# Half of x's channel pairs come from DRAM as 32x32 blocks and are turned by DVE; TensorE turns the other half

## The chip, the cores and the metric

The kernel runs on one core of a Trainium2 chip. The metric is the device time of one execution, in microseconds (us), as the median of three runs.

The engines are named as the profile names them: PE (TensorE, with PEld for its weight loads), ACT (ScalarE), DVE (VectorE), POOL (GpSimd) and SP (SyncE, which here only issues DMAs). Each works through its own instructions in the order in which they are written, and semaphores tie them together.

## What is computed

A hybrid layer for 256 tokens and 4096 channels in float32: a norm, one wide projection, three mixers (a gated mLSTM, a sparse attention, a gated delta rule), and an output projection that is added to x.

```python
h = rms_norm(x, norm_g[l])
proj = jnp.einsum('bsd,dn->bsn', h, w_in[l])
(aq, ak, av, ai, af, ao, az,
 bcq, bk, bv, bki, bwi, bz,
 cqkv, cb, ca, cz) = jnp.split(proj, split_points, axis=-1)
...
y = jnp.concatenate([y_a, y_b, y_c], axis=-1)
x = x + jnp.einsum('bsm,md->bsd', y, w_out[l])
```

What concerns the change is only how x comes to stand as the stationary operand of the first matrix multiplication: with channels on the 128 partitions and tokens along the free dimension. In DRAM x lies the other way round, tokens by channels.

## The kernel before, in words

All weights are streamed once from DRAM in **chunks** of 128 channels by 1024 numbers (512 KB, two groups of 128 channels by 512 columns). Each chunk goes through three engines. SP loads it into `w_raw` (four buffers). ACT copies it, rounded to a shorter float, into `w_hi` (`split_hi`). DVE subtracts to get the remainder `w_lo` (`split_lo`). PE then multiplies in three products, `hi*hi`, `hi*lo` and `lo*hi`, which makes twelve matmuls of 128x512 per chunk (lines 825 to 827). Sixteen chunks make one block of 512 output columns; the blocks follow each other to the end of the kernel, and the mixers' work is woven in between their chunks.

The operand of these matmuls, `op_hi` and `op_lo`, holds h transposed, 32 groups of 128 channels by 256 tokens. It is made during the first block. This stretch, from the start to about 59 us, is called the **x phase** here. x is loaded by SP in pieces into `xs`, tokens on partitions. For each pair of channel groups i (16 pairs, one for each chunk of the first block), four steps follow:

- `x_columns(i)` on PE: four transposes of 128x128 from `xs` into a PSUM bank `mix` (they appear as line 798);
- `x_hi(i)` on ACT: two copies of 128x256 from the bank, times the norm's gain, into `op_hi` (line 1391);
- `x_lo(i)` on DVE: two operations of 128x256 that read the bank and `op_hi` and write `op_lo` (line 1915);
- chunk i on PE, which waits for `x_lo(i)` and for `split_lo(i)`.

The order on each engine is fixed by the loops over chunks c. On PE it is `chunk(c)`, then `x_columns(c + 2)`. On ACT it is `x_hi(c + 2)`, `split_hi(c + 3)`, `x_square(c)` (a square of 128x512 with a running sum, for the norm). On DVE it is `x_lo(c + 2)`, `split_lo(c + 3)`. One round of the loops is called a **slot**, and slot i is the one in which ACT runs `x_hi(i)`, then `split_hi(i + 1)`. `split_hi(c)` also waits for the load of chunk c and for PE to have finished chunk c - 4; SP issues the load of chunk c when `split_lo(c - 4)` is done.

POOL makes a few constants in the first 5 us and then has nothing to do until the first block is finished; after that it moves tiles through DRAM scratch in blocks of 32x32 numbers (`keep_blocks`, `bring_blocks`), and DVE turns those blocks in place (`STREAM_TRANSPOSE`). The scratch moves of `conv`, `v`, `lane` and the others are of this kind.

Of the kernel before, what the change touches and what calls it, by code (L numbers as in the profile page):

```python
# [17 lines left out]
ACT = mybir.ActivationFunctionType  # L18
AX_X = mybir.AxisListType.X

P = 128
D = 4096
SEQ = 256
# [45 lines left out]
AHEAD = SPLIT_BUFS - 1  # L69
X_AHEAD = 2  # L70
NX = KT // 2
X_PARTS = [(q, q + SEQ) for q in range(0, 1024, SEQ)] + [(q, q + 512) for q in range(1024, D, 512)]
WARM = (2, 2, 1)
RSQRT = 1597463007.0
# [150 lines left out]
def hybrid_kernel(nc, x, norm_g, w_in, w_out, m_ib, m_fb, m_norm_g, a_cq_g, a_wuq, a_wuqi, a_qn_g, a_kn_g,  # L225
                  a_ki_g, a_ki_b, d_conv_w, d_a_log, d_dt_bias, d_norm_g, out):
    blocks, chunks, last, woven, _ = plan()
    U0 = NX + 1

    matrix = {  # L230
        "w_in": w_in[0].rearrange("(kt p) n -> p kt n", p=P),
# [7 lines left out]
    with ExitStack() as ctx:  # L239
# [3 lines left out]
        def sem(name):  # L243
            return ctx.enter_context(nc.semaphore(name))
# [11 lines left out]
        op_hi = sb("op_hi", [P, KT, SEQ], F32R)  # L256
        op_lo = sb("op_lo", [P, KT, SEQ], F32R)
# [89 lines left out]
        x_ready = [sem(f"x_ready{q}") for q in range(len(X_PARTS))]  # L347
        raw_ready = [sem(f"raw_ready{b}") for b in range(RAW_BUFS)]
        const_ready = sem("const_ready")
        pool_step = sem("pool_step")  # L350
        head_ready = sem("head_ready")
        x_hi_ready = sem("x_hi_ready")
# [115 lines left out]
        def first_half(tensor, i):  # L468
            w = blocks[0]["width"]
            return tensor[:, 0, i * w:i * w + w]  # L470

        def first_bank(j):

# [11 lines left out]
        def bank(use):  # L485
            return mix[use % 4]

        def wait_filled(eng, use):
            eng.wait_ge(filled[use % 4], use // 4 + 1)
# [116 lines left out]
        def _(pool):  # L606
# [24 lines left out]
            for i, lv in enumerate(MERGES):  # L631
                b = 1 << lv
# [3 lines left out]
                select(v, ALU.is_ge, 0.0, -b, [[-2 * b, n], [0, b]], 1)  # L636
                select(v, ALU.is_ge, 0.0, 2 * b - 1, [[2 * b, n], [0, b]], -1)
            nc.gpsimd.engine_nop().then_inc(const_ready, 1)

            def clear_corners(m):  # L640

# [151 lines left out]
        def _(pe):  # L793
# [6 lines left out]
            def chunk(c):  # L800
                b, kts = chunks[c]
                blk = blocks[b]
                w = blk["width"]
                if kts[0] == blk["kts"][0] and b >= 2:
                    pe.wait_ge(acc_read[b % 2], b // 2)
                pe.wait_ge(lo_ready, c + 1)
                hi, lo = {"h": (op_hi, op_lo), "cq": (cq_hi, cq_lo), "y": (op_hi, op_lo)}[blk["operand"]]
                hv = split_ap(w_hi, c).rearrange("p (k n) -> p k n", k=len(kts))
                lv = split_ap(w_lo, c).rearrange("p (k n) -> p k n", k=len(kts))
                if c == len(chunks) - 1:  # L810
                    order = [(i, kt, [m]) for m in range(M) for i, kt in enumerate(kts)]
                else:
                    order = [(i, kt, range(M)) for i, kt in enumerate(kts)]
                for i, kt, ms in order:
                    if b == 0:
                        use = 1 + kt // 2
                        pe.wait_ge(emptied[use % 4], use // 4 + 1)
                    if blk["operand"] == "cq":
                        pe.wait_ge(cq_lo_ready, kt // 2 + 1)
                    if blk["kind"] in ("out1", "out2") and blk["arg"] == 0:  # L820
                        pe.wait_ge(y_lo_ready, (kt // 2 + 12) % 16 + 1)
                    for m in ms:
                        o = acc[b % 2][m][:, 0:w]
                        tok = slice(m * P, m * P + P)
                        nc.tensor.matmul(o, hi[:, kt, tok], hv[:, i, :], start=(kt == blk["kts"][0]), stop=False)  # L825
                        nc.tensor.matmul(o, hi[:, kt, tok], lv[:, i, :], start=False, stop=False)  # L826
                        last_mm = nc.tensor.matmul(o, lo[:, kt, tok], hv[:, i, :], start=False,  # L827
                                                   stop=(kt == blk["kts"][-1]))
                        if c == len(chunks) - 1 and m == 0 and kt == kts[-1]:
                            last_mm.then_inc(last_half, 1)  # L830
                if c == last[b]:
                    last_mm.then_inc(acc_ready, 1)
                    pe_done[0] += 1
                else:
                    last_mm.then_inc(split_used, 1)
# [201 lines left out]
            def second_chunk(c):  # L1037

                w = blocks[0]["width"]
                hv = split_ap(w_hi, c).rearrange("p (k n) -> p k n", k=2)  # L1040
                lv = split_ap(w_lo, c).rearrange("p (k n) -> p k n", k=2)
                use = 1 + c
                pe.wait_ge(emptied[use % 4], use // 4 + 1)
                pe.wait_ge(hi_ready, c + 1)
                for part, op in ((hv, op_hi), (hv, op_lo), (lv, op_hi)):
                    if part is lv:
                        pe.wait_ge(lo_ready, c + 1)
                    for i in range(2):
                        for m in range(M):
                            ins = nc.tensor.matmul(acc[0][m][:, 0:w], op[:, 2 * c + i, m * P:m * P + P],  # L1050
                                                   part[:, i, :], start=False, stop=False)
                ins.then_inc(split_used, 1)
# [4 lines left out]
                    nc.tensor.matmul(bank(3)[:, 0:P], ident[:], ident[:], start=True, stop=True)  # L1057

            def x_columns(i):
                use = 1 + i  # L1060
                pe.wait_ge(x_ready[i if i < 4 else i // 2 + 2], 16)
                wait_emptied(pe, use)
                for j in range(2):
                    for m in range(M):
                        o = first_bank(j) if i == 0 else bank(use)[:, j * SEQ:j * SEQ + SEQ]
                        ins = turn(o[:, m * P:m * P + P], xs[:, m, (2 * i + j) * P:(2 * i + j) * P + P])
                    if i == 0 and j == 0:
                        ins.then_inc(first_turned, 1)
                end_fill(ins, use)
# [12 lines left out]
            for c in range(1, len(chunks)):  # L1082
                if c < 3:
                    second_chunk(c)
                else:
                    chunk(c)
                if c + X_AHEAD < NX:
                    x_columns(c + X_AHEAD)
                if c == NX:
                    pe.wait_ge(const_ready, 2)  # L1090
                for name, arg, use in woven[c]:
                    if name in pieces:
                        pieces[name](arg, U0 + use)


        @block.scalar
        def _(act):
# [286 lines left out]
                          bs=bs, bp=bp, ae=ae, ap=ap, yt=yt)  # L1384

            def x_hi(i):
                use = 1 + i
                wait_filled(act, use)
                for j in range(2):
                    kt = 2 * i + j  # L1390
                    ins = func(op_hi[:, kt, :], bank(use)[:, j * SEQ:j * SEQ + SEQ], ACT.Copy,
                               scale=par[:, R_NORM + kt:R_NORM + kt + 1])
                ins.then_inc(x_hi_ready, 1)

            def x_square(i):
                q, m = i // M, i % M
                for part in ((0, 1), (2, 3))[q] if q < 2 else (q + 2,):
                    act.wait_ge(x_ready[part], 16)
                func(y[:, m, 512 * q:512 * q + 512], xs[:, m, 512 * q:512 * q + 512], ACT.Square,
                     accum_out=ssq[:, m, q:q + 1]).then_inc(ss_ready, 1)  # L1400

            def first_x(j):
# [43 lines left out]
        def _(dve):  # L1446
# [9 lines left out]
            def done_bank(ins, use):  # L1456
                ins.then_inc(emptied[use % 4], 1)
# [443 lines left out]
            def par_columns(_, use):  # L1901
                for i, (c0, n) in enumerate(((R_CQ, R_N - R_CQ), (R_N, N_TAP))):
# [4 lines left out]
                          co=co, cy=cy, bn=bn, bt=bt, bkn=bkn, bkt=bkt, bit=bit, bqn=bqn, bqt=bqt, bsc=bsc, btk=btk, bts=bts, bs=bs, bo=bo, at=at, ae=ae, ap=ap, ay=ay,  # L1907
                          yd=yd, yt=yt)

            def x_lo(i):  # L1910
                use = 1 + i
                dve.wait_ge(x_hi_ready, i + 1)
                for j in range(2):
                    kt = 2 * i + j
                    ins = vec.scalar_tensor_tensor(op_lo[:, kt, :], bank(use)[:, j * SEQ:j * SEQ + SEQ],
                                                   par[:, R_NORM + kt:R_NORM + kt + 1], op_hi[:, kt, :].bitcast(F32),
                                                   ALU.mult, ALU.subtract)
                done_bank(ins, use)

            wait_filled(dve, 0)  # L1920
            done_bank(vec.tensor_copy(par[:, 0:R_CQ], bank(0)[:, 0:R_CQ]), 0)
# [14 lines left out]
            for c in range(len(chunks)):  # L1936
                if 0 < c < NX - X_AHEAD:
                    x_lo(c + X_AHEAD)
                if c + AHEAD < len(chunks):
                    split_lo(c + AHEAD)  # L1940
                if c == NX - 1:
                    dve.wait_ge(ss_ready, NX)
                    step(vec.tensor_reduce(rstd[:], ssq[:], AX_X, ALU.add))
                    rsqrt_mean(rstd[:], D, rstd_ready)
                    dve.wait_ge(const_ready, 2)
                for name, arg, use in woven[c]:
                    if name in pieces:
                        pieces[name](arg, U0 + use)
# [26 lines left out]
```

## Time and profile before

| | us |
|---|---|
| median of three runs | 1555.44 |
| lowest and highest | 1554.95, 1555.63 |
| the profiled execution's own time | 1556.13 |
| its span, first to last instruction | 1554.4 |

PE's clock is granted in full over the whole span (the page shows 9, that is 90% or more, in each of 40 slices). The profile's rows are read as: start, duration, engine, line, what is written from what, count; in brackets the idle time ahead of the row and what ended it. A row with x2 or x4 covers that many instructions, and its duration is their total. Instructions of one engine overlap by about 0.1 us, so the distance between two starts is the time that the first one takes of its engine. The groups have the busy time in us, the mean duration of one in ns, and the idle time ahead of them.

### The profile page before, as it was taken

How to read it: one execution, taken by the hardware profiler on the slowest of the kernel's cores; microseconds unless marked ns; L12 is line 12 of the kernel's file. 1: busy time of each engine (PE TensorE's matmuls, PEld its weight loads, DVE VectorE, ACT ScalarE, POOL GpSimd, SP SyncE). 2: the span in 40 equal slices, each digit the busy share in tenths (PEclk: the TensorE clock that was granted, in tenths of full speed). 3: DMA queues.
4: the chain of work that ended last, by engine and by line, in shares of the span. 5: the costliest groups of instructions: out<-in, count | busy, mean ns of one | idle time of the engine just before them, and what ended most of it. 6: DMA issues, size and time to landing. Idle time of an engine off the chain costs nothing.

```text
span 1554.4 us, 18886 instructions
## 1 busy us (share of the span) xinstructions
PE 1548.2 (100%) x7124; PEld 1281.0 (82%) x7124; DVE 979.9 (63%) x1503; ACT 757.6 (49%) x1022; POOL 292.8 (19%) x492
## 2 busy tenths in 40 slices
PE   9999999999999999999999999999999999999999
PEld 7888888888888888888878888888888888888887
DVE  5665555666759854566579666665456776665554
ACT  6654444487544444554545545544445444444332
POOL 0121112230020030026610241333500110100000
PEclk9999999999999999999999999999999999999999
DMA  8677778886687675468856765676875766666674
GB/s 295 209 211 219 214 221 225 211 234 193 200 231 209 196 218 157 130 189 271 257 182 180 221 211 174 211 234 202 281 214 179 256 205 196 202 206 194 193 250 153
DMA packets 179095, 327.74 MB, mean 211 GB/s; under 512 B 29346, under 2 KB 34612, under 8 KB 178876
## 3 DMA queue, kind: packets, MB, share of 16 engines
q1 hardware_dynamic: 161324, 284.00, 60.7%
q0 software_dynamic: 17632, 42.52, 9.6%
q8 instruction: 56, 0.92, 0.2%
q14 instruction: 35, 0.29, 0.1%
q10 hardware_dynamic: 48, 0.02, 0.0%
HBM read 307.05 MB, written 19.42 MB: 210 GB/s over the span
## 4 chain that ended last, share of the span: by engine, by line
PE 97%; DVE 1%; ACT 1%; issue 0%; DMA 0%; ACTq 0%
PE acc L825 31%; PE acc L827 30%; PE acc L826 30%; PE mix L897 1%; PE mix L798 1%; PE mix L981 1%; PE mix L879 0%; DVE w_lo L1462 0%; PE mix L962 0%; PE acc L1050 0%; ACT w_hi L1120 0%; PE mix L959 0%; PE mix L949 0%; PE mix L947 0%; PE mix L991 0%
## 5 line engine op out<-in xcount | busy, mean ns | idle before, releaser
L1462 DVE TENSOR_TENSOR w_lo<-w_raw,w_hi 128x1024 fp32r<-128x1024 f32 (+2 forms) x535 | 645.9, 1217 | 427.7 <-ACT w_hi L1120 424.1
L825 PE MATMUL acc<-w_hi,op_hi 128*128 128x512 f32 (+1 forms) x2036 | 802.5, 394 | 0.3 <-DVE w_lo L1462 0.3
L1120 ACT ACTIVATE w_hi<-w_raw 128x1024 fp32r<-128x1024 f32 (+2 forms) x535 | 556.0, 1050 | 504.7 <-PE acc L827 452.9
L827 PE MATMUL acc<-w_hi,op_lo 128*128 128x512 f32 (+1 forms) x2036 | 793.4, 390 | 0.0
L826 PE MATMUL acc<-w_lo,op_hi 128*128 128x512 f32 (+1 forms) x2036 | 792.3, 389 | 0.0
L827 PEld LDWEIGHTS acc<-w_hi,op_lo 128*128 128x128 f32 x2036 | 382.1, 188 | 81.0
L825 PEld LDWEIGHTS acc<-w_hi,op_hi 128*128 128x128 f32 x2036 | 382.4, 188 | 80.4 <-DVE w_lo L1462 2.7
L826 PEld LDWEIGHTS acc<-w_lo,op_hi 128*128 128x128 f32 x2036 | 382.5, 188 | 76.6
L650 POOL DMA_DIRECT2D y_dram<-y x64 | 41.0, 713 | 211.1 <-DVE y L1877 115.2
L650 POOL DMA_DIRECT2D conv_dram<-y x48 | 30.9, 703 | 207.5 <-ACT y L1172 206.8
L650 POOL DMA_DIRECT2D bq_dram<-qs x32 | 20.4, 676 | 158.4 <-DVE qs L1751 157.9
L658 POOL DMA_DIRECT2D y<-y_dram x64 | 33.9, 538 | 34.5 <-DMA y_dram<-y 34.0
L1344 ACT ACTIVATE b_p<-b_s,st 128x128 f32<-128x128 f32 (+1 forms) x32 | 14.3, 446 | 52.9 <-DVE st L1824 52.9
L825 PE MATMUL acc<-w_hi,cq_hi 128*128 128x512 f32 x84 | 33.7, 401 | 0.0
L826 PE MATMUL acc<-w_lo,cq_hi 128*128 128x512 f32 x84 | 33.1, 394 | 0.0
L827 PE MATMUL acc<-w_hi,cq_lo 128*128 128x512 f32 x84 | 33.1, 394 | 0.0
L658 POOL DMA_DIRECT2D y<-conv_dram x48 | 25.5, 542 | 22.9 <-DMA conv_dram<-y 22.9
L1593 DVE SCALAR_TENSOR_TENSOR cT<-y,par,cT 128x255 f32<-128x255 f32 (+2 forms) x72 | 29.4, 476 | 0.0
L788 POOL DMA_DIRECT2D out_dram<-acc x2 | 1.5, 731 | 124.6 <-DVE acc L1485 124.6
L711 POOL DMA_DIRECT2D lane_out_dram<-lane_u x4 | 4.2, 1068 | 108.2 <-DVE lane_u L1651 108.2
L1651 DVE TENSOR_TENSOR lane_u<-lane_u,lane_t 128x252 f32<-128x252 f32 (+52 forms) x63 | 22.4, 356 | 2.2
L1222 ACT ACTIVATE cT<-cT 128x512 f32<-128x512 f32 x12 | 7.6, 633 | 33.1 <-DVE cT L1593 33.1
(326 smaller groups left out, 927.3 us busy)
## 6 DMA issues: line engine op xcount, KB each, us to landing
w_raw<-in_w_in_dram SPq DMA_DIRECT2D x367, 512.0 KB, 4.4
w_raw<-in_w_out_dram SPq DMA_DIRECT2D x128, 512.0 KB, 4.6
w_raw<-in_w_in_dram SPq DMA_DIRECT2D x16, 384.0 KB, 3.2
w_raw<-in_a_wuq_dram SPq DMA_DIRECT2D x12, 512.0 KB, 4.9
y_dram<-y POOLq DMA_DIRECT2D x64, 64.0 KB, 4.2
y<-y_dram POOLq DMA_DIRECT2D x64, 64.0 KB, 3.5
xs<-in_x_dram SPq DMA_DIRECT2D x6, 512.0 KB, 5.1
conv_dram<-y POOLq DMA_DIRECT2D x48, 64.0 KB, 3.8
```

The costliest lines, as they stand in the source:

```text
L650: pool.dma_start(dst[:, :, :, 4 * m + i, :].rearrange("a k j b -> a (k j) b"), src[32 * i:32 * i + 32, m].rearrange("p (f b) -> p f b", b= ...
L658: pool.dma_start(dst[32 * j:32 * j + 32, q].rearrange("p (k t) -> p k t", k=2), src[:, 2 * q:2 * q + 2, j].rearrange("a k i b -> a k (i b) ...
L798: return nc.tensor.transpose(dst, src, ident[0:n, 0:n])
L825: nc.tensor.matmul(o, hi[:, kt, tok], hv[:, i, :], start=(kt == blk["kts"][0]), stop=False)
L826: nc.tensor.matmul(o, hi[:, kt, tok], lv[:, i, :], start=False, stop=False)
L827: last_mm = nc.tensor.matmul(o, lo[:, kt, tok], hv[:, i, :], start=False, stop=(kt == blk["kts"][-1]))
L897: ins = nc.tensor.matmul(bank(use)[:, a * n:a * n + n], lhs(a), rhs(a), start=True, stop=True)
L981: ins = nc.tensor.matmul(bank(use)[:, o * P:o * P + P], b_pT[:, i, :], val, start=(v == 0 or i % 2 == 0), stop=(v == 0 or i % 2 == 1))
L1120: func(split_ap(w_hi, c), w_raw[:, c % RAW_BUFS, 0:n], ACT.Copy).then_inc(hi_ready, 1)
L1462: vec.tensor_tensor(split_ap(w_lo, c), w_raw[:, c % RAW_BUFS, 0:n], split_ap(w_hi, c).bitcast(F32), ALU.subtract).then_inc(lo_ready, 1)
L1593: ins = vec.scalar_tensor_tensor(cT[:, c, d:SEQ], conv_columns(i, j)[:, 0:SEQ - d], par[:, row:row + 1], cT[:, c, d:SEQ], ALU.mult, ALU.add)
L1651: ins = vec.tensor_tensor(done, done, t, ALU.subtract)
```

## The change

Of the 16 pairs, eight (5, 6, 8, 9, 11, 12, 14, 15) are "moved": PE does not transpose them any more. POOL issues 64 more DMAs behind its constants, eight for each moved pair, that read x again from DRAM, 32 tokens by 32 channels at a time, so that each 32x32 block stands in the right place but is not turned. Each DMA brings 32 KB in runs of 128 bytes into a stage that lies in `y`. DVE turns a pair's blocks with one `STREAM_TRANSPOSE` of 128x512 in place (`x_turn`), in its loop behind `split_lo` of the same chunk. `x_hi` and `x_lo` of these pairs read the stage instead of a PSUM bank. The squares are written to `kv` instead of `y`; nothing reads them. SP still loads all of x, since the squares and the other eight pairs need it.

```diff
+X_MOVED = [c for c in range(5, NX) if c % 3 != 1]
+X_TURNED = [c for c in range(NX) if c not in X_MOVED]
...
-    U0 = NX + 1
+    U0 = len(X_TURNED) + 1
...
+        def x_stage(c):
+
+            n = X_MOVED.index(c)
+            return y[:, n % 2, 512 * (n // 2):512 * (n // 2) + 512]
...
+        def wait_x(eng, c):
+
+            if c in X_MOVED:
+                eng.wait_ge(x_lo_ready, X_MOVED.index(c) + 1)
+            else:
+                eng.wait_ge(emptied[x_use(c) % 4], x_use(c) // 4 + 1)
...
             nc.gpsimd.engine_nop().then_inc(const_ready, 1)
+
+            for n, c in enumerate(X_MOVED):
+                for i in range(2):
+                    for j in range(4):
+                        col = P * (2 * c + i) + 32 * j
+                        pool.dma_start(
+                            x_stage(c)[32 * j:32 * j + 32, SEQ * i:SEQ * i + SEQ].rearrange("p (f a) -> p f a", a=32),
+                            x[0][:, col:col + 32].rearrange("(f b) a -> b f a", b=32)).then_inc(x_moved[n], 16)
...
                     if b == 0:
-                        use = 1 + kt // 2
-                        pe.wait_ge(emptied[use % 4], use // 4 + 1)
+                        wait_x(pe, kt // 2)
...
-                if c + X_AHEAD < NX:
+                if c + X_AHEAD in X_TURNED:
                     x_columns(c + X_AHEAD)
...
             def x_hi(i):
-                use = 1 + i
-                wait_filled(act, use)
+                if i in X_MOVED:
+                    act.wait_ge(x_turned, X_MOVED.index(i) + 1)
+                else:
+                    wait_filled(act, x_use(i))
...
-                func(y[:, m, 512 * q:512 * q + 512], xs[:, m, 512 * q:512 * q + 512], ACT.Square,
+                func(kv[:, m, 512 * (q % 2):512 * (q % 2) + 512], xs[:, m, 512 * q:512 * q + 512], ACT.Square,
...
+            def x_turn(c):
+                n = X_MOVED.index(c)
+                dve.wait_ge(x_moved[n], 16 * 8)
+                vec.transpose(x_stage(c), x_stage(c)).then_inc(x_turned, 1)
...
                 if c + AHEAD < len(chunks):
                     split_lo(c + AHEAD)
+                if c + X_AHEAD + 1 in X_MOVED:
+                    x_turn(c + X_AHEAD + 1)
```

On PE the transposes between chunk 3 and chunk 4 are gone, and so are those behind chunk 4. Before, from the last matmul of chunk 3 to the first of chunk 5:

```order
L827 MATMUL acc<-w_hi,op_lo 128x512
L798 MATMUL mix<-ident,xs 128x128 [waits emptied2,x_ready4]
L798 MATMUL mix<-ident,xs 128x128 x3
L825 MATMUL acc<-w_hi,op_hi 128x512 [waits emptied1,lo_ready]
...
L827 MATMUL acc<-w_hi,op_lo 128x512
L798 MATMUL mix<-ident,xs 128x128 [waits emptied3,x_ready5]
L798 MATMUL mix<-ident,xs 128x128 x3
L825 MATMUL acc<-w_hi,op_hi 128x512 [waits emptied2,lo_ready]
```

Now, over the same stretch (the lines have moved by 30; between the dots stand only matmuls of a chunk):

```order
L857 MATMUL acc<-w_hi,op_lo 128x512
L855 MATMUL acc<-w_hi,op_hi 128x512 [waits emptied1,lo_ready]
...
L857 MATMUL acc<-w_hi,op_lo 128x512
L855 MATMUL acc<-w_hi,op_hi 128x512 [waits x_lo_ready,lo_ready]
```

Four transposes are gone ahead of chunk 4 and four ahead of chunk 5, and chunk 5 waits for DVE's new semaphore instead of a bank's. The same happens in six more places.

On DVE, at the slots of pairs 4 to 6, the rows before are `x_lo(4)`, `split_lo(5)`, `x_lo(5)`, `split_lo(6)`, `x_lo(6)`:

```order
L1915 SCALAR_TENSOR_TENSOR op_lo<-mix1,par,op_hi 128x256
L1462 TENSOR_TENSOR w_lo<-w_raw,w_hi 128x1024 [waits hi_ready]
L1915 SCALAR_TENSOR_TENSOR op_lo<-mix2,par,op_hi 128x256 [waits x_hi_ready]
L1915 SCALAR_TENSOR_TENSOR op_lo<-mix2,par,op_hi 128x256
L1462 TENSOR_TENSOR w_lo<-w_raw,w_hi 128x1024 [waits hi_ready]
L1915 SCALAR_TENSOR_TENSOR op_lo<-mix3,par,op_hi 128x256 [waits x_hi_ready]
```

Now a transpose stands behind `split_lo(5)` and another behind `split_lo(6)`:

```order
L1950 SCALAR_TENSOR_TENSOR op_lo<-mix1,par,op_hi 128x256
L1493 TENSOR_TENSOR w_lo<-w_raw,w_hi 128x1024 [waits hi_ready]
L1944 STREAM_TRANSPOSE y<-y 128x512 [waits x_moved0]
L1950 SCALAR_TENSOR_TENSOR op_lo<-y,par,op_hi 128x256 [waits x_hi_ready]
L1950 SCALAR_TENSOR_TENSOR op_lo<-y,par,op_hi 128x256
L1493 TENSOR_TENSOR w_lo<-w_raw,w_hi 128x1024 [waits hi_ready]
L1944 STREAM_TRANSPOSE y<-y 128x512 [waits x_moved1]
L1950 SCALAR_TENSOR_TENSOR op_lo<-y,par,op_hi 128x256 [waits x_hi_ready]
```

On ACT the order is as it was; only the wait ahead of the copies of pair 5 has moved from PE (`filled2`) to DVE (`x_turned`), which stands here with the split behind it:

```order
L1422 ACTIVATE op_hi<-y,par 128x256 [waits x_turned]
L1422 ACTIVATE op_hi<-y,par 128x256
L1149 ACTIVATE w_hi<-w_raw 128x1024 [waits split_used,raw_ready2]
L1430 ACTIVATE kv,ssq<-xs 128x512 [waits x_ready3,x_ready2]
L1422 ACTIVATE op_hi<-y,par 128x256 [waits x_turned]
```

What moved is the source of the wait: pair 5's copies stand behind a DVE operation that itself stands behind the split of the slot before.

## Rows read from the trace of the kernel before

**Rows 1.** The page: busy time by engine, and the chain that ended last.

```profile
PE 1548.2 (100%) x7124; PEld 1281.0 (82%) x7124; DVE 979.9 (63%) x1503; ACT 757.6 (49%) x1022; POOL 292.8 (19%) x492
...
PE 97%; DVE 1%; ACT 1%; issue 0%; DMA 0%; ACTq 0%
```

**Rows 2.** Timeline of PE: start us, us, engine, line, operation, tiles, count.

```profile
27.76 0.60 PE L798 MATMUL mix<-ident,xs 128*128 128x128 f32 x4
...
30.97 0.60 PE L798 MATMUL mix<-ident,xs 128*128 128x128 f32 x4
31.33 0.48 PE L825 MATMUL acc<-w_hi,op_hi 128*128 128x512 f32 x1
...
56.67 0.39 PE L825 MATMUL acc<-w_hi,op_hi 128*128 128x512 f32 x1
...
62.55 0.39 PE L825 MATMUL acc<-w_hi,op_hi 128*128 128x512 f32 x1
...
65.28 0.39 PE L825 MATMUL acc<-w_hi,op_hi 128*128 128x512 f32 x1
```

**Rows 3.** Timeline of ACT: one slot of the x phase, two squares, the last slot.

```profile
18.77 0.84 ACT L1391 ACTIVATE op_hi<-mix,par 128x256 fp32r<-128x256 f32 x2 [0.79 <-PE mix L798]
19.50 1.06 ACT L1120 ACTIVATE w_hi<-w_raw 128x1024 fp32r<-128x1024 f32 x1
20.45 0.63 ACT L1399 ACTIVATE y<-xs 128x512 f32<-128x512 f32 x1
...
54.10 0.84 ACT L1391 ACTIVATE op_hi<-mix,par 128x256 fp32r<-128x256 f32 x2 [0.82 <-PE mix L798]
...
57.34 0.62 ACT L1399 ACTIVATE y<-xs 128x512 f32<-128x512 f32 x1
57.95 0.62 ACT L1399 ACTIVATE y<-xs 128x512 f32<-128x512 f32 x1
```

**Rows 4.** Timeline of DVE: the same slot and the last one.

```profile
19.65 0.87 DVE L1915 SCALAR_TENSOR_TENSOR op_lo<-mix,par,op_hi 128x256 fp32r<-128x256 f32 x2 [1.01 <-ACT op_hi L1391]
20.59 1.23 DVE L1462 TENSOR_TENSOR w_lo<-w_raw,w_hi 128x1024 fp32r<-128x1024 f32 x1
...
54.97 0.88 DVE L1915 SCALAR_TENSOR_TENSOR op_lo<-mix,par,op_hi 128x256 fp32r<-128x256 f32 x2 [1.04 <-ACT op_hi L1391]
```

**Rows 5.** Timeline of DVE: a transpose of blocks behind a split.

```profile
91.11 1.23 DVE L1462 TENSOR_TENSOR w_lo<-w_raw,w_hi 128x1024 fp32r<-128x1024 f32 x1 [1.49 <-ACT w_hi L1120]
92.25 0.70 DVE L1585 STREAM_TRANSPOSE y<-y 128x512 f32<-128x512 f32 x1
```

**Rows 6.** Timeline of ACT: two copies from y ahead of a split.

```profile
1203.17 0.89 ACT L1378 ACTIVATE op_hi<-y,par 128x256 fp32r<-128x256 f32 x2
1203.97 1.04 ACT L1120 ACTIVATE w_hi<-w_raw 128x1024 fp32r<-128x1024 f32 x1
```

**Rows 7.** POOL: end of its constants, then groups with mean ns of one.

```profile
4.74 0.55 POOL L616 TENSOR_SCALAR_AFFINE_SELECT level<-level 128x64 bf16<-128x64 bf16 x2
...
L676 POOL DMA_DIRECT2D cT<-v_dram x8 | 4.6, 588 | 10.9 <-DMA v_dram<-cT 10.9
L705 POOL DMA_DIRECT2D lane_right<-lane_in_dram x4 | 4.2, 1056 | 5.1 <-DMA lane_in_dram<-y 5.1
```

**Rows 8.** DMA in 441 to 460 us: queues, then issues with median us to landing.

```profile
q0 software_dynamic: 512, 1.57, 39.3%
...
w_raw<-in_w_in_dram SPq DMA_DIRECT2D x6, 512.0 KB, 9.2
lane_right<-lane_in_dram POOLq DMA_DIRECT2D x4, 256.0 KB, 7.8
```

**Rows 9.** Windows: PE, PEld, DVE, ACT, POOL busy, clock, DMA share, GB/s.

```profile
10.00:18.40 8.40, 8.26 (x42) 6.63 (x42) 7.02 (x10) 7.52 (x14) 0.00 (x0) 1.00 0.97 341
```

**Rows 10.** SP's issues, and the landing of the one begun in 13.0 to 14.5 us.

```profile
8.01 5.61 SPq L569 DMA_DIRECT2D w_raw<-in_w_in_dram  x2
...
w_raw<-in_w_in_dram SPq DMA_DIRECT2D x1, 512.0 KB, 4.0
```

More of the change, by code:

```diff
@@ L349, in hybrid_kernel @@
         const_ready = sem("const_ready")
+        x_moved = [sem(f"x_moved{n}") for n in range(len(X_MOVED))]
+        x_turned = sem("x_turned")
+        x_lo_ready = sem("x_lo_ready")
         pool_step = sem("pool_step")
@@ L470, in first_half, with x_use, x_source @@
             return tensor[:, 0, i * w:i * w + w]
+        def x_use(c):
+            return 1 + X_TURNED.index(c)
+        def x_stage(c):
+            n = X_MOVED.index(c)
+            return y[:, n % 2, 512 * (n // 2):512 * (n // 2) + 512]
+        def x_source(c):
+            return x_stage(c) if c in X_MOVED else bank(x_use(c))
+        def wait_x(eng, c):
[3 more added lines that the diff above has]
+                eng.wait_ge(emptied[x_use(c) % 4], x_use(c) // 4 + 1)
         def first_bank(j):
@@ L1041, in second_chunk @@
                 lv = split_ap(w_lo, c).rearrange("p (k n) -> p k n", k=2)
-                use = 1 + c
-                pe.wait_ge(emptied[use % 4], use // 4 + 1)
+                wait_x(pe, c)
                 pe.wait_ge(hi_ready, c + 1)
@@ L1059, in x_columns @@
             def x_columns(i):
-                use = 1 + i
+                use = x_use(i)
                 pe.wait_ge(x_ready[i if i < 4 else i // 2 + 2], 16)
@@ L1386, in x_hi @@
             def x_hi(i):
-                use = 1 + i
-                wait_filled(act, use)
+                if i in X_MOVED:
+                    act.wait_ge(x_turned, X_MOVED.index(i) + 1)
+                else:
+                    wait_filled(act, x_use(i))
                 for j in range(2):
                     kt = 2 * i + j
-                    ins = func(op_hi[:, kt, :], bank(use)[:, j * SEQ:j * SEQ + SEQ], ACT.Copy,
+                    ins = func(op_hi[:, kt, :], x_source(i)[:, j * SEQ:j * SEQ + SEQ], ACT.Copy,
                                scale=par[:, R_NORM + kt:R_NORM + kt + 1])
@@ L1908, in _ @@
                           yd=yd, yt=yt)
+            def x_turn(c):
+                n = X_MOVED.index(c)
+                dve.wait_ge(x_moved[n], 16 * 8)
+                vec.transpose(x_stage(c), x_stage(c)).then_inc(x_turned, 1)
             def x_lo(i):
-                use = 1 + i
                 dve.wait_ge(x_hi_ready, i + 1)
@@ L1914, in x_lo @@
                     kt = 2 * i + j
-                    ins = vec.scalar_tensor_tensor(op_lo[:, kt, :], bank(use)[:, j * SEQ:j * SEQ + SEQ],
+                    ins = vec.scalar_tensor_tensor(op_lo[:, kt, :], x_source(i)[:, j * SEQ:j * SEQ + SEQ],
                                                    par[:, R_NORM + kt:R_NORM + kt + 1], op_hi[:, kt, :].bitcast(F32),
                                                    ALU.mult, ALU.subtract)
-                done_bank(ins, use)
+                if i in X_MOVED:
+                    ins.then_inc(x_lo_ready, 1)
+                else:
+                    done_bank(ins, x_use(i))
             wait_filled(dve, 0)
```

## The prediction

> **What bounds the kernel now.** I read the page first. PE is busy for 1548.2 us of a span of 1554.4, and it is 97% of the chain that ended last [rows 1]. So PE's time is the kernel's time, and a change that only touches the first 60 us moves the end by what it moves PE's first block, and by nothing else. The question is then where the last chunks of the x phase start.
>
> The timelines of the three engines give the slot. On PE the transposes of one pair start at 27.76 and of the next at 30.97: a slot lasts 3.21 us, with no idle time [rows 2]. The transposes hold PE for 0.36 us up to the first matmul behind them (30.97 to 31.33). A chunk with no transposes around it takes 2.73 us (62.55 to 65.28), which makes 0.48 with the small loss around them. ACT starts `x_hi(4)` at 18.77, `split_hi(5)` at 19.50, the square at 20.45, and then sits idle 0.8 us until PE has turned the next pair [rows 3]. DVE waits about 1 us for ACT in each slot [rows 4]. So before the change only PE is full, and the other two follow it.
>
> **What is removed.** Eight times four transposes. If nothing else bound the phase, PE would gain 8 x 0.36 = 2.9 us to 8 x 0.48 = 3.8 us.
>
> **What is added, and where it stands.** DVE gets eight `STREAM_TRANSPOSE`s of 128x512. A same one takes 0.70 us and starts 1.14 us after the split ahead of it [rows 5]. DVE has 3.21 us a slot and uses about 2.1, so the 0.70 fit by their sum. They do not fit by their place. Before, `x_hi(i)` waited for PE, which was ahead of everybody. Now it waits for `x_turn(i)`, which stands behind `split_lo(i)`, which waits for `split_hi(i)`, which ACT runs behind `x_hi(i - 1)`. That is a closed chain from one `x_hi` to the next, through two engines:
>
> - `x_hi(i - 1)` up to the start of `split_hi(i)`: 0.73 us from PSUM [rows 3], 0.80 us from `y` [rows 6];
> - `split_hi(i)`: 1.06; hand-over to DVE: 19.50 + 1.06 = 20.56 to 20.59, so 0.03 [rows 3, 4];
> - `split_lo(i)` up to the start of `x_turn(i)`: 1.14; the transpose 0.70 [rows 5]; hand-over back, taken as the same 0.03.
>
> The sum is 3.69 us behind a pair from PSUM and 3.76 behind a moved one. Both are longer than the 3.21 us that a slot had, and much longer than the 2.73 that PE now needs. A pair that PE still turns has no such wait: its `x_hi` follows the one before it as soon as ACT is free, after 0.80 + 0.95 (`split_hi` to the square, 19.50 to 20.45) + 0.61 (square to the next instruction, 57.34 to 57.95) = 2.36 us [rows 3, 6].
>
> The pattern of pairs is two moved, one turned: 3.69 + 3.76 + 2.36 = 9.81 us for three slots. Before, three slots took 3 x 3.21 = 9.63; PE alone would now want 9.63 - 2 x 0.48 = 8.67. So the chain decides, PE waits about 1.1 us in every three slots, and the eight pairs' gain is gone.
>
> In time: `x_hi(4)` is the last start that PE sets as before, 18.77. Up to `x_hi(15)` there are three triples and one pair of moved ones: 18.77 + 3 x 9.81 + 3.69 + 3.76 = 55.65, against 54.10 before [rows 3]. PE had 0.8 us in hand there: `x_lo(15)` ended at 54.97 + 0.88 = 55.85 and chunk 15 started at 56.67 [rows 2, 4]. Now chunk 15 starts as soon as `x_lo(15)` is done: 55.65 + 0.89 + 0.03 + 0.87 + 0.03 = 57.47, which is 0.80 us later than 56.67. Behind chunk 15 everything is as before. Term one: +0.8 us.
>
> **POOL's 64 DMAs.** POOL is free from 5.3 us. Issuing a DMA of the same make (32 partitions by 8 runs each) takes 0.588 us, one of 2048 runs 1.056 [rows 7]. At 0.588 the last is issued at 5.3 + 64 x 0.588 = 42.9. As landing time I take the longest of a kind with short runs, 7.8 us [rows 8]. Then the first pair's eight are there at 5.3 + 4.7 + 7.8 = 17.8, and `x_turn(5)` can start at 19.50 + 1.06 + 0.03 + 1.14 = 21.7; the last eight are there at 50.7, and `x_turn(15)` stands at 55.65 - 0.73 = 54.9. So the new waits of DVE cost nothing, with some 4 us in hand at either end.
>
> **What these DMAs do to the others.** This is the unknown. The trace has one stretch in which POOL's queue reads DRAM in runs of 128 bytes, 441 to 460 us [rows 8]: 1.57 MB, or 12,270 runs, took 39.3% of 16 engines for 19 us, so 9.7 ns a run. The 64 DMAs have 16,384 runs: 10 us of all 16 engines, at 256 x 9.7 / 16 = 0.155 us per 0.588 us, a share of 26%, until about 43 us. Between 10.0 and 18.4 us the DMA engines are already full, at 0.97 [rows 9], so here the share comes out of the loads' time: 26% of the 8 us from 5.3 to 13.3 is 2.1 us of backlog. The load that matters is that of chunk 5: issued at 13.62 - 0.37 = 13.25 (the end of the second issue, less what one takes), landed 4.0 later at 17.3 [rows 10], used by ACT at 19.50 [rows 3]. It has 2.2 us in hand, about what the backlog takes. Anything beyond that goes straight into the chain. From below the cost is 0; from above it is what rows 8 show beside a saturated queue, a landing of 9.2 us: 13.25 + 9.2 - 19.50 = 2.9 us. I take 0.4, near the lower end, because POOL issues a run four times more slowly here than in rows 8 (0.588 us for 256, there 1.056 for 2048). Term two: +0.4 us.
>
> The squares' new target and the source of `x_lo` in `y` cost nothing: they are the same shapes on the same engines, and DVE's 0.87 is hidden behind ACT's split.
>
> **The sum.** +0.8 + 0.4 = +1.2 us. The profiled execution's own time of 1556.13 would become 1557.3. The median of the runs is 0.69 below that execution, 1555.44, and becomes 1556.6. A measurement of this kernel can tell about 0.2% from no change, 3.1 us; this is within it.
>
> **The rivals.**
>
> - *PE gets its gain.* It would need the chain of 3.7 us to be shorter than PE's own time. For that, each hand-over through DVE would have to lose 0.57 us (9.81 against 8.67, over two moved slots). Nothing in rows 3 to 6 leaves room: the durations repeat to 0.01 us. What speaks for it is only that DVE and ACT are busy far less than PE. Time: 1555.44 - 2.9 to - 3.8, so 1551.6 to 1552.5. Chance 0.06.
> - *The load of chunk 5 is late (slower).* It is this one load, as the loads behind it gain slack with each slot. It costs from a landing of 6.3 us on (19.50 - 13.25), and over 0.2% from 8.6; at 9.2 us the time is 0.8 + 2.9 = +3.7, 1559.1, and a little more if chunk 4's load is late as well. For it speaks the DMA share of 0.97 there; against it, the low rate of issue. Chance of more than +3.1 us: 0.12.
> - *POOL is too slow.* It decides from (54.9 - 5.3 - 7.8) / 64 = 0.65 us a DMA on. At 0.75 us it would be 64 x 0.10 = +6 us, at the 1.056 of rows 7 +26 us. Chance 0.05.
> - *The reads are far dearer.* A pair's 256 KB at the 341 GB/s of rows 9 is 0.77 us of all engines, and by the runs of rows 8 it is 1.24. If it were tens of microseconds, DMA would bound the whole phase. By runs of this length nothing points to that. Chance 0.01.
>
> The Trainium skill, "DMA: Bandwidth & Descriptors", section "Rules for kernel authors", speaks against this change: it says that transposing by a plain DMA with a rearranged access pattern is 19 times slower than the hardware's DMA transpose. As an estimate from that page's factor, 0.77 us would become some 15 us a pair, and the time about 60 us longer or more. The rows here show a factor of 1.6 for runs of 128 bytes, not 19, and only the order inside the block is left to DVE; that is why the last rival has 0.01.
>
> The Trainium skill, "SBUF — State Buffer", section "Who interferes with whom", would feed the third rival: a VectorE instruction in a two-port mode keeps GpSimd from writing its descriptors. Whether a transpose of float32 is one, no row here shows.
>
> **How the numbers follow.** The forecast, the chain with a small share of late loads, has 0.76: 1555.9 (no late load, hand-overs a little shorter) to 1558.5. Slower by over 0.2% are the second to fourth rivals, 0.18; faster by over 0.2% is most of the first, 0.05; the rest, 0.77, is within. The range for 8 in 10 leaves out the gain and the far ends of the slower ones: 1554.6 to 1559.6. Its lower end allows for the chain being 0.25 us a moved slot shorter than added up.
>
> **What would show it.** Right: in the profile after, ACT's idle time ahead of `x_hi` of a moved pair ends with DVE's transpose, not with PE or DMA; the starts of `x_hi` are 3.7, 3.8 and 2.4 us apart; PE waits for DVE's `op_lo` ahead of the chunks of moved pairs, about 1.1 us in three slots; chunk 15 starts near 57.5 to 58. POOL's groups show near 0.6 us a DMA. Wrong: if DVE's transpose waits for a DMA, POOL or the queue is the bound; if `split_hi(5)` waits for its load by more than 0.5 us, term two is too small; if PE has no waits in the phase, the chain is not there.

## The result, and the profile after

The changed kernel takes 1558.86 us (median of 13 runs, 1558.31 to 1560.29), against 1555.64 (13 runs, 1554.79 to 1556.25) for the kernel before on the same chip. The ratio is 1.0022, 95% interval 1.0015 to 1.003: 3.2 us slower, where 1.2 was forecast and the range ended at 1559.6. By the bound of 0.2% that the prediction set (3.1 us), this is just on the slower side. The profiled execution took 1558.31, against 1556.13 before.

The page after answers to [rows 1]. PE's share of the last chain has fallen from 97% to 94%, and DVE's has grown from 1% to 3%:

```profile
PE 1545.5 (99%) x7092; PEld 1276.7 (82%) x7092; DVE 984.9 (63%) x1511; ACT 758.1 (49%) x1022; POOL 329.5 (21%) x556
...
PE 94%; DVE 3%; ACT 2%; DMA 1%; issue 1%; ACTq 0%; DVEq 0%
```

The waits of the first 65 us (who waited for whom: us in total, times, longest) name both costs. The first two rows are the chain through DVE, the third is the loads:

```profile
ACT op_hi L1422 <- DVE y L1944: 10.4, 8, 1.3
PE acc L855 <- DVE op_lo L1950: 4.4, 9, 0.8
ACT w_hi L1149 <- DMA w_raw<-in_w_in_dram: 2.7, 2, 1.3
```

The timeline of ACT shows the chain directly; it answers to [rows 3] and [rows 6]:

```profile
17.59 1.06 ACT L1149 ACTIVATE w_hi<-w_raw 128x1024 fp32r<-128x1024 f32 x1 [1.32 <-DMA w_raw<-in_w_in_dram]
...
19.17 0.82 ACT L1422 ACTIVATE op_hi<-mix,par 128x256 fp32r<-128x256 f32 x2
...
22.84 0.91 ACT L1422 ACTIVATE op_hi<-y,par 128x256 fp32r<-128x256 f32 x2 [1.31 <-DVE y L1944]
...
26.63 0.91 ACT L1422 ACTIVATE op_hi<-y,par 128x256 fp32r<-128x256 f32 x2 [1.30 <-DVE y L1944]
...
29.00 0.81 ACT L1422 ACTIVATE op_hi<-mix,par 128x256 fp32r<-128x256 f32 x2
```

The starts of `x_hi` are 3.67, 3.79 and 2.37 us apart; 3.69, 3.76 and 2.36 had been added up. The first row is the other cost: `split_hi(4)` waits 1.32 us for its load, in a slot ahead of every moved pair. Chunk 15 on PE, which answers to [rows 2], now starts behind a wait for its operand, at 58.11 instead of 56.67:

```profile
58.11 0.47 PE L855 MATMUL acc<-w_hi,op_hi 128*128 128x512 f32 x1 [0.77 <-DVE op_lo L1950]
```

The windows (columns as in [rows 9]) show the DMA engines full (a share of 1.06) through the whole stretch in which POOL issues. The kernel before had 0.97, 0.92, 0.75 and 0.60 in the same four windows:

```profile
10.00:18.40 8.40, 8.26 (x43) 6.61 (x42) 5.89 (x9) 5.68 (x10) 8.40 (x16) 1.00 1.06 315
18.40:31.30 12.90, 11.05 (x49) 8.36 (x48) 10.11 (x15) 10.30 (x23) 12.90 (x23) 1.00 1.06 321
31.30:44.20 12.90, 12.14 (x54) 9.25 (x52) 9.66 (x15) 8.99 (x20) 10.97 (x20) 1.00 1.06 322
44.20:57.00 12.80, 11.82 (x52) 9.27 (x52) 9.57 (x14) 8.90 (x21) 0.00 (x0) 1.00 0.78 221
```

The DMA view of 0 to 60 us has the price of it: a weight load now lands 8.0 us after its issue, where the same view of the kernel before has 4.2. The third row is POOL's own group from the page, answering to [rows 7]:

```profile
w_raw<-in_w_in_dram SPq DMA_DIRECT2D x20, 512.0 KB, 8.0
...
y<-in_x_dram POOLq DMA_DIRECT2D x64, 32.0 KB, 5.5
...
L667 POOL DMA_DIRECT2D y<-in_x_dram x64 | 36.9, 585 | 0.1
```

### The profile page after: what moved, and what is told of

Same layout as the page of the kernel before. It is cut to its first block, busy times and chain, and to the rows that moved or that the text cites. A ratio compares the mean times of both kernels' runs of the same rounds, so it can differ in the third digit from the quotient of the medians.

```text
span 1556.5 us, 18886 instructions
## 1 busy us (share of the span) xinstructions
PE 1545.5 (99%) x7092; PEld 1276.7 (82%) x7092; DVE 984.9 (63%) x1511; ACT 758.1 (49%) x1022; POOL 329.5 (21%) x556
## 4 chain that ended last, share of the span: by engine, by line
PE 94%; DVE 3%; ACT 2%; DMA 1%; issue 1%; ACTq 0%; DVEq 0%
PE acc L855 30%; PE acc L857 30%; PE acc L856 29%; PE mix L927 1%; DVE w_lo L1493 1%; ACT w_hi L1149 1%; PE mix L829 1%; PE mix L1011 1%; DMA w_raw<-in_w_in_dram 1%; PE mix L909 0%; ACT op_hi L1422 0%; PE mix L992 0%; DVE y L1944 0%; PE mix L989 0%; PE mix L979 0%
## 5 line engine op out<-in xcount | busy, mean ns | idle before, releaser
L689 POOL DMA_DIRECT2D y<-y_dram x64 | 33.9, 538 | 35.4 <-DMA y_dram<-y 34.8
L667 POOL DMA_DIRECT2D y<-in_x_dram x64 | 36.9, 585 | 0.1
```

Source lines behind the costliest of these rows:

```text
L667: pool.dma_start(x_stage(c)[32 * j:32 * j + 32, SEQ * i:SEQ * i + SEQ].rearrange("p (f a) -> p f a", a=32), x[0][:, col:col + 32].rearrang ...
L689: pool.dma_start(dst[32 * j:32 * j + 32, q].rearrange("p (k t) -> p k t", k=2), src[:, 2 * q:2 * q + 2, j].rearrange("a k i b -> a k (i b) ...
```

## The experiments

The theory (T1): the time is the sum of two costs, the chain through DVE and the late loads. Each median stands against the kernel before on the same chip, which was 1555.74 (27 runs) beside the first four kernels and 1555.61 (26 runs) beside the other four. These differ by 0.1 us, and so much of every difference between two kernels may come from where they ran. The 95% intervals of most ratios below reach about 1.4 us to either side, so a difference of less than that isn't shown by the medians alone.

### turn_early: the turn ahead of the split

On DVE the two conditions change places, so that `x_turn(i)` no longer stands behind `split_lo(i)` and with it behind ACT.

```diff
+                if c + X_AHEAD + 1 in X_MOVED:
+                    x_turn(c + X_AHEAD + 1)
                 if c + AHEAD < len(chunks):
                     split_lo(c + AHEAD)
-                if c + X_AHEAD + 1 in X_MOVED:
-                    x_turn(c + X_AHEAD + 1)
```

> The changed kernel with one swap on DVE: x_turn(i) stands ahead of split_lo(i) instead of behind it; nothing else differs. Theory 1, the closed chain x_hi, split_hi, split_lo, x_turn, x_hi: the chain now is x_hi, x_lo, x_turn, about 2.4 us a slot, shorter than PE's 2.73, so PE has no waits for op_lo in the slots from 6 on and gets back 8 x 0.36 to 8 x 0.48 us; with the late loads at the start staying, the time is 1552 to 1554. Theory 2, the DMA engines are the bound of the phase (their share is 1.06 from 18 to 44 us): the order on DVE does not matter, the time stays within 1 us of the changed kernel, 1558 to 1559, and the waits move to w_raw.

Measured: 1555.95 (11 runs), ratio 1.0002 [0.9993, 1.0011]. That is 2.9 us less than the changed kernel, and between the times of the two theories. The wait of `x_hi` for DVE is gone; another stands in its place. The waits of 0 to 65 us, and ACT's rows around `split_hi(4)`:

```profile
ACT w_hi L1149 <- DMA w_raw<-in_w_in_dram: 10.8, 8, 2.1
...
PE acc L855 <- DVE op_lo L1950: 3.3, 4, 1.3
```

```profile
19.05 1.06 ACT L1149 ACTIVATE w_hi<-w_raw 128x1024 fp32r<-128x1024 f32 x1 [1.92 <-DMA w_raw<-in_w_in_dram]
20.62 0.82 ACT L1422 ACTIVATE op_hi<-mix,par 128x256 fp32r<-128x256 f32 x2
23.00 0.91 ACT L1422 ACTIVATE op_hi<-y,par 128x256 fp32r<-128x256 f32 x2
```

From a pair of PE's to a moved one it is now 2.38 us instead of 3.67. With the chain out of the way, ACT reaches every split sooner and the loads are what it waits for, 10.8 us in eight instead of 2.7 in two. So the chain had hidden part of what the DMAs cost. Nor is that cost only at the start: of PE's four waits two are at 18.2 and 22.5 us, but one of 1.23 us is at 35.4, behind a split that waited 1.79 us for its load.

### no_block_dmas: the chain without the DMAs

POOL fills the stages with a constant instead of loading them, so half of the first operand is not x. All else stands.

```diff
             for n, c in enumerate(X_MOVED):
-                for i in range(2):
...
+                nc.gpsimd.memset(x_stage(c), 0.5).then_inc(x_moved[n], 1)
```

> The changed kernel without its 64 DMAs: POOL fills each stage by a memset, so the moved half of x's channels is not read and the output is made from a constant there; DVE still turns, the order is kept. Theory 1 (the chain sets the slots, the DMAs only cost at the start): x_hi(4) starts near 18.8 instead of 19.17, the spacing of 3.7, 3.8 and 2.4 us stays, and the time is 0.4 to 1.4 us below the changed kernel, 1557.4 to 1558.5, still slower than before. Theory 2 (the DMA engines are the bound): the kernel is faster than before by 3 us, about 1552.

Measured: 1556.57 (11 runs), ratio 1.0006 [0.9997, 1.0015]: +0.83 us, where term one was +0.80. The interval runs from about -0.5 to +2.3 us. The pattern is that of theory 1, its time isn't: 2.3 us below the changed kernel instead of 0.4 to 1.4, so the DMAs cost more than it allowed them. The starts of `x_hi` on ACT:

```profile
17.68 0.84 ACT L1417 ACTIVATE op_hi<-mix,par 128x256 fp32r<-128x256 f32 x2 [0.78 <-PE mix L824]
21.37 0.91 ACT L1417 ACTIVATE op_hi<-y,par 128x256 fp32r<-128x256 f32 x2 [1.30 <-DVE y L1939]
25.15 0.91 ACT L1417 ACTIVATE op_hi<-y,par 128x256 fp32r<-128x256 f32 x2 [1.30 <-DVE y L1939]
27.52 0.82 ACT L1417 ACTIVATE op_hi<-mix,par 128x256 fp32r<-128x256 f32 x2
```

3.69, 3.78, 2.37: the same chain, with no DMA of POOL's in it. From `x_hi(4)` to chunk 15 on PE it is 38.92 us here (17.68 to 56.60), 38.94 in the changed kernel (19.17 to 58.11) and 37.90 before (18.77 to 56.67). So in the traces the chain costs 1.0 us, with or without the DMAs. A weight load lands in 4.3 us.

### before_plus_dmas: the DMAs without the chain

PE turns all 16 pairs as before; POOL issues the 64 DMAs into `y`, where nothing reads them. The squares go to `kv`, with a wait for the buffer, and ACT waits for the DMAs before the first write of its own to `y`, long after.

```diff
+X_MOVED = [c for c in range(5, NX) if c % 3 != 1]
...
+                        pool.dma_start(
+                            x_stage(c)[32 * j:32 * j + 32, SEQ * i:SEQ * i + SEQ].rearrange("p (f a) -> p f a", a=32),
+                            x[0][:, col:col + 32].rearrange("(f b) a -> b f a", b=32)).then_inc(x_moved[n], 16)
```

> The kernel before, with the 64 DMAs added behind POOL's constants; nobody reads the blocks, PE turns all 16 pairs, and the squares go to kv. It prices the DMAs where PE has 0.8 to 1.2 us in hand in each slot. Theory 1: the loads of chunks 3 and 4 are late as in the changed kernel, ACT takes it up in its idle time, and the time is within 0.5 us of before, 1555.5 to 1556.2. Theory 2: 2 us or more slower than before.

Measured: 1557.33 (11 runs), ratio 1.0011 [1.0002, 1.002]: +1.6 us, between the two theories. By the medians the DMAs alone cost time even where PE is full. ACT waits for loads, which land in 9.0 us:

```profile
ACT w_hi L1135 <- DMA w_raw<-in_w_in_dram: 8.6, 7, 1.9
```

In the profiled execution (1556.59) ACT's waits ate only what it had in hand over PE, and PE shows none of its own. Most of the timed runs lost more than it, and no trace shows where.

### turn_thrice: the suspected link made longer

```diff
+                step(vec.transpose(x_stage(c), x_stage(c)))
+                step(vec.transpose(x_stage(c), x_stage(c)))
                 vec.transpose(x_stage(c), x_stage(c)).then_inc(x_turned, 1)
```

Three transposes in place leave the stage as one does.

> The changed kernel with each stage turned three times in place instead of once (the result is that of one turn). Theory 1: the closed chain becomes longer by two transposes and their hand-overs, 1.4 to 1.5 us in each of eight slots, so 11 to 12 us slower than the changed kernel, about 1570. Theory 2 (DVE's idle time, about 1 us a slot, can take up more work): under 4 us slower.

Measured: 1572.79 (4 runs), ratio 1.0108 [1.0093, 1.0124], 13.9 us over the changed kernel. `x_hi` of a moved pair waits up to 2.8 us for DVE, and its slot lasts 5.26 us (25.84 to 31.10) instead of 3.77, so the chain takes all that is put in. The rest goes with the clock. In the profiled execution chunk 15 starts 13.38 us later than in the changed kernel's: 1.50 of it are there already at `x_hi(4)` (20.67 against 19.17), and 11.88 are the eight stretched slots, as expected. Then chunk 15 itself takes 4.75 us up to chunk 16 (71.49 to 76.24) instead of 3.16 (58.11 to 61.27), 1.6 us more; with the 11.9 of the slots that makes 13.5 of the 13.9. It starts behind a wait of 2.26 us, and the granted clock, which was 1.00 there in the changed kernel, is 0.73 and 0.69:

```profile
71.49 0.47 PE L855 MATMUL acc<-w_hi,op_hi 128*128 128x512 f32 x1 [2.26 <-DVE op_lo L1952]
...
76.24 0.48 PE L855 MATMUL acc<-w_hi,op_hi 128*128 128x512 f32 x1
```

```profile
70.00:74.00 4.00, 2.51 (x7) 2.03 (x8) 3.14 (x4) 4.00 (x10) 0.00 (x0) 0.73 0.22 56
74.00:76.00 2.00, 2.00 (x8) 1.31 (x6) 0.87 (x2) 1.29 (x5) 0.00 (x0) 0.69 0.78 244
```

### turn_early_no_dmas: both costs removed

The edits of `turn_early` and `no_block_dmas` together, so again with a constant in place of half of x.

```diff
+                nc.gpsimd.memset(x_stage(c), 0.5).then_inc(x_moved[n], 1)
...
+                if c + X_AHEAD + 1 in X_MOVED:
+                    x_turn(c + X_AHEAD + 1)
                 if c + AHEAD < len(chunks):
                     split_lo(c + AHEAD)
```

> Both suspected costs taken away at once: x_turn ahead of split_lo, and POOL fills the stages by memsets instead of the 64 DMAs (the moved half of x's channels is a constant). Theory 1 (the closed chain and the block DMAs are the only two things that eat PE's gain): no wait of PE for op_lo from chunk 5 on, and the full gain of 8 x 0.36 to 8 x 0.48 us below the kernel before, 1552.0 to 1553.0. Rival (something else in the changed kernel costs too, such as restarts of PE or the copies from y): 1554 or more.

Measured: 1551.93 (10 runs), ratio 0.9976 [0.9967, 0.9985]: 3.7 us faster than before, which is 0.07 us beyond the times of theory 1. This is the whole of what the prediction gave for the removed transposes, 2.9 to 3.8. It also leaves nothing for the copies from `y` to cost. Whether restarts of PE cost something can't be seen here, as it no longer stops. PE has no wait for `op_lo`, and ACT waits for PE again:

```profile
18.77 0.84 ACT L1417 ACTIVATE op_hi<-mix,par 128x256 fp32r<-128x256 f32 x2 [0.82 <-PE mix L824]
21.17 0.92 ACT L1417 ACTIVATE op_hi<-y,par 128x256 fp32r<-128x256 f32 x2
23.69 0.91 ACT L1417 ACTIVATE op_hi<-y,par 128x256 fp32r<-128x256 f32 x2
27.42 0.84 ACT L1417 ACTIVATE op_hi<-mix,par 128x256 fp32r<-128x256 f32 x2 [1.25 <-PE mix L824]
```

Three slots are 8.65 us (18.77 to 27.42), where the prediction put PE alone at 8.67.

### long_runs: the same bytes in runs of 2 KB

Sixteen DMAs of 128 KB bring other numbers of x, in long runs, to the same stages; the chain stays.

```diff
-                    for j in range(4):
...
+                    pool.dma_start(x_stage(c)[64 * i:64 * i + 64, :],
+                                   x[0][128 * i + 64:128 * i + 128, 256 * (c - 1):256 * (c - 1) + 512]).then_inc(x_moved[n], 16)
```

> The changed kernel with its 64 DMAs replaced by 16 that bring the same 2 MB in runs of 2 KB (64 rows of 512 channels each; the numbers in the stages are then the wrong ones). The chain is kept. Theory 1 (what costs is the engines' time for runs of 128 bytes): the loads of chunks 3 and 4 are less late, and the time is 1 to 2 us below the changed kernel, 1557 to 1558. Theory 2 (what costs is the bytes, or that a second queue takes turns with SP's): within 0.5 us of the changed kernel, 1558.4 to 1559.4.

Measured: 1565.59 (5 runs), ratio 1.0063 [1.0051, 1.0076], 6.7 us slower than the changed kernel. Both theories missed. POOL's row, then the waits, show why:

```profile
5.40 8.45 POOL L665 DMA_DIRECT2D y<-in_x_dram  x16
```

```profile
ACT w_hi L1146 <- DMA w_raw<-in_w_in_dram: 9.3, 3, 6.6
...
PE mix L826 <- DMA xs<-in_x_dram: 5.7, 2, 3.5
```

POOL is done issuing at 13.85 us instead of 42.28, so all 2 MB compete with the first loads of weights and of x itself. One split waits 6.6 us. All three splits wait 9.3 us together, 6.6 more than the changed kernel's 2.7, which is about the whole difference. The granted clock also fell here, to 0.74 in 18.4 to 31.3 us, but that cost nothing that can be seen: from `x_hi(5)` to chunk 15 it is 35.25 us (30.44 to 65.69), and 35.27 in the changed kernel. Long runs alone are no remedy, then: 2.10 MB took 13.0% of the queues' time in 0 to 60 us here, and 11.8% in the changed kernel. The run changes two things at once, the length of the runs and how fast POOL hands out the bytes, so it doesn't price short runs by themselves. It does fit that the slow issue, 0.585 us for 32 KB, had kept the changed kernel's cost small.

### six_pairs_at_once and six_pairs_later: fewer pairs, then a later start

Both have the early turn and move only pairs 8, 9, 11, 12, 14 and 15, which leaves room for the transfers to start later. The second lets POOL wait until ACT has split chunk 3.

```diff
-X_MOVED = [c for c in range(5, NX) if c % 3 != 1]
+X_MOVED = [c for c in range(8, NX) if c % 3 != 1]
...
+            pool.wait_ge(hi_ready, 4)
             for n, c in enumerate(X_MOVED):
```

> The same with POOL's 48 DMAs right behind its constants, at 5.4 us. Theory 1 (the cost lies at the start): 1 to 1.5 us slower than with the later start. Theory 2 (the cost lies all through the phase): the same as with the later start, within 0.5 us.

> x_turn ahead of split_lo; moved pairs are 8, 9, 11, 12, 14, 15 only, and POOL starts its 48 DMAs when ACT has split chunk 3, near 15 us, so that the first loads have the DMA engines for themselves. Theory 1 (the block DMAs cost at the start only, where loads have no time in hand): PE gets 6 x 0.36 to 6 x 0.48 us, 1552.9 to 1553.7. Theory 2 (they cost all through the phase): PE still waits in the slots behind 25 us, 1554.5 or more.

Measured: 1554.35 (11 runs), ratio 0.9992 [0.9983, 1.0001] at once; 1553.18 (11 runs), ratio 0.9984 [0.9975, 0.9992] with the later start. The 48 DMAs are the same; only when they start differs, and it is worth 1.2 us. The two intervals overlap, but of the eleven runs at once ten are above every run with the later start. At once, ACT waits 7.9 us for loads in the first 65 us; later, it waits for two, 0.17 and 0.52 us, and PE is busy in every microsecond of the windows, with DMA at 1.05 and 1.06 beside it:

```profile
ACT w_hi L1149 <- DMA w_raw<-in_w_in_dram: 7.9, 5, 2.1
```

```profile
18.40:31.30 12.90, 12.90 (x66) 10.63 (x64) 8.53 (x14) 10.07 (x22) 12.90 (x23) 1.00 1.05 314
31.30:44.20 12.90, 12.90 (x61) 10.65 (x60) 11.32 (x19) 11.44 (x24) 11.70 (x21) 1.00 1.06 299
```

So in this execution a full DMA share cost PE nothing, with loads that land in 6.8 us. (It is one that began slowly, and the one at once began fast, in the sense of the last section; the medians don't hang on that pair.) This version leaves nothing out, and is 2.4 us faster than the kernel before and 5.7 faster than the changed one.

## Why the prediction was right and wrong

**The chain (term one, +0.80): right, shown.** Its links are in the rows and the three distances above hold to 0.03 us, all of it is gone with the early turn when no DMA stands behind it, and three transposes stretch it by 1.49 us a slot, as they should. Its size is 1.0 us in the traces and +0.83 by the medians; with an interval of 1.4 us to either side, that the second meets 0.80 so closely is luck. One reading was off: PE's rows show waits of 0.7 us in three slots (0.35 at 44.52, 0.33 at 48.29), not 1.1, though the three slots last 9.82 us (38.47 to 48.29), where 9.81 had been added up.

**The gain that it eats: right, shown.** The removed transposes are worth 3.7 us (predicted 2.9 to 3.8). From `turn_early_no_dmas` to `no_block_dmas`, only the chain is added, and it costs 3.7 + 0.8 = 4.5 us.

**POOL keeps up: right.** 0.585 us a DMA against 0.588; the last is issued at 42.28, predicted 42.9; they land in 5.5 us, where 7.8 was allowed. DVE's transposes show no wait for a DMA.

**The DMAs' effect on the others (term two, +0.4): this is the step that failed, in its size and in its place.** By medians it is 1558.86 - 1555.64 less 0.83, so 2.4 with the chain, 1.6 on the kernel before, and 3.9 with the early turn (0.2 over the kernel before against 3.7 under it). Three parts of the step were off:

- The load named was that of chunk 5. It was not waited for. Those of chunks 3 and 4 were, 1.35 and 1.32 us: they are issued sooner, when the slots have little in hand. The prediction named chunk 4 only in passing, as "a little more". Its sign for a term two that is too small, a wait of `split_hi(5)`, therefore did not show, though the term was too small.
- The backlog was put at a share of 26%, until 13.3 us, against a load with 2.2 us in hand. The landing of a load went from 4.2 to 8.0 us over the whole phase, and the share to 1.06. The upper bound of 9.2 us [rows 8] was nearly right, and the value taken was near the lower one.
- The reason given for the low value, that POOL issues slowly, fits the 6.7 us of `long_runs`, but it was not enough to make the cost small.

**The sum.** 1558.86 is above 1558.5, where the forecast's own band ended, and inside the range only by the room that was left for late loads. It is also made up otherwise than added: both costs together take 3.7 + 3.2 = 6.9 us from the gain, where 4.5 for the chain alone and 3.9 for the DMAs alone would make 8.4. So T1 holds for the two causes, not for their plain sum.

**The profiled execution hid part of it.** Its `x_hi(4)` starts at 19.17, 0.40 later than 18.77 before, just term two. But this execution had begun faster, for the reason in the last section. Beside `no_block_dmas`, which began fast as well, `x_hi(4)` is 19.17 - 17.68 = 1.49 us late, chunk 15 is 58.11 - 56.60 = 1.51 late, and the two executions' own times are 1558.31 - 1556.53 = 1.8 apart. So of the 2.4 us, 1.5 are traced to the loads of chunks 3 and 4.

**What stays open.** The rest, up to 0.9 us, isn't traced, and it is less than the medians resolve. Between the profiles of before and after, the distance at chunk 16 is 1.53 us (61.27 against 59.74) and at the last operation of DVE 1.77. The difference arises at 403 us, where a stretch of PE takes 2.21 us (402.94 to 405.15) instead of 1.93 (401.41 to 403.34), and nothing here says whether it belongs to the change. For `before_plus_dmas` the medians show 1.6 us, while its profiled execution is 0.5 over that of before; which load was late in the other executions can't be seen.

**The rivals.** PE does not get its gain by this order, as said; it gets it when the turn stands early and the loads are not late. The second rival, late loads and more than +3.1 us, had 0.12, and by its time (+3.2) it is what came, through the loads of chunks 3 and 4 instead of that of chunk 5. The rule of the Trainium skill, "DMA: Bandwidth & Descriptors", section "Rules for kernel authors" (transposing by a plain DMA with a rearranged pattern 19 times slower than by the hardware's transpose), did not reach this change: these DMAs keep runs of 128 bytes and leave the turning to DVE. The 2.10 MB took 11.8% of the queues' time in 0 to 60 us, 7.1 us of all 16 engines, where 10 were estimated. No DMA that transposes was run here, so the rule itself isn't tested.

## What to carry to other kernels

Add up not only an engine's work per slot but the loop from one instruction back to itself through the in-order engines: here ACT, DVE and ACT again took 3.7 us for a slot in which neither was busy for more than 3, and changing the order of two instructions removed it. Work taken from the bound engine and given to a DMA queue is paid first by the transfers that have no slack; find the earliest load that is used as soon as it lands, and start the new transfers behind it. Two costs in one stretch don't simply add (6.9 us here for 4.5 and 3.9), since one hides part of the other: take them away one at a time and both together.

## What had not been expected of the hardware

PE's matmuls begin slow and change at a time that differs between executions, while the granted clock of 6.4 to 9.1 us is 1.00 in both kernels' windows. In the kernel before, pairs of 128x512 matmuls take 1.05 us up to about 9.3 us and follow each other every 0.85; in the execution after they take 0.63 from 7.34 on, one every 0.46. The timeline of PE, before and then after:

```profile
7.40 1.05 PE L1030 MATMUL acc<-w_hi,op_lo 128*128 128x512 f32 x2
8.25 1.05 PE L1033 MATMUL acc<-w_lo,op_hi 128*128 128x512 f32 x2
```

```profile
7.34 0.63 PE L1060 MATMUL acc<-w_hi,op_lo 128*128 128x512 f32 x2
7.80 0.62 PE L1063 MATMUL acc<-w_lo,op_hi 128*128 128x512 f32 x2
```

Of the ten profiled executions four changed early and six late, and kernels with the same instructions up to there fall in both groups (the changed kernel changed early, `turn_thrice` late), so it does not come from the change. It shifts the first slots by 1.1 us (`x_hi(4)` at 17.68 or 18.77), which is as much as the effects studied here. Two profiles should first be compared at this place.

Beside a second queue that reads 2 MB in short runs, the loads of 512 KB took 7.7 to 9.0 us to land instead of 4.2, and all queues together moved hardly more, or less. In 10.0 to 18.4 us the changed kernel moved 315 GB/s with a DMA share of 1.06, the kernel before 341 with 0.97 [rows 9], and `no_block_dmas`, which began as fast as the changed kernel, 401 with 1.05:

```profile
10.00:18.40 8.40, 8.26 (x43) 6.69 (x42) 7.25 (x10) 7.39 (x14) 0.00 (x0) 1.00 1.05 401
```

So a full share doesn't say how much is moved: in this stretch two queues moved fewer bytes than one. In 18.4 to 31.3 us it was 321 against 307 before. Why is open; long runs don't cure it, as `long_runs` moved 275 GB/s in the first of these windows.
